# The inverse of a chunked scan by head groups, with its first products on four 64x64 tiles

## The reference

```
def step(S, inp):
    r_t, w_t, k_t, v_t, kk_t, b_t = inp
    sa = jnp.einsum('bhvk,bhk->bhv', S, -kk_t)
    S = (S * w_t[:, :, None, :] + sa[..., None] * b_t[:, :, None, :]
         + v_t[..., None] * k_t[:, :, None, :])
    y_t = jnp.einsum('bhvk,bhk->bhv', S, r_t)
    return S, y_t
```

## Time and profile before

| | |
|---|---|
| median of 3 runs | 1394.27 us (1393.8 to 1395.25) |
| profiled execution | 1393.7 us, its span 1391.9 us |
| busy, share of the span | PE 98%, weight loads 84%, DVE 68%, ACT 54%, POOL 5% |
| granted TensorE clock, mean | 0.999 of full speed |
| the scan's levels and joins | 101 to 135 us and 161 to 186 us |

### The profile page before, as it was taken

One profiled execution on the slowest core, in us unless ns is written; L12 is line 12 of the kernel. 1 busy time (PEld: TensorE's weight loads), 2 busy tenths in 40 slices (PEclk: granted clock), 3 DMA queues, 4 the chain that ended last, 5 costly groups with the idle time before them and its releaser, 6 DMA issues.

```text
span 1391.9 us, 23527 instructions
## 1 busy us (share of the span) xinstructions
PE 1363.1 (98%) x9838; PEld 1175.4 (84%) x9838; DVE 950.7 (68%) x1480; ACT 748.2 (54%) x1262; POOL 62.7 (5%) x63
## 2 busy tenths in 40 slices
PE   6999999999999999999999999999999999999998
PEld 6789888888889778888889877888888898788886
DVE  7896786766675776756667544577666697767665
ACT  6873434555456575545453446555555536555543
POOL 0003440000010000000000000000000100000000
PEclk9999999999999999999999999999999999999999
DMA  9421006555554415555565543545555653455551
GB/s 333 158 72 33 4 27 241 188 185 188 202 205 161 144 49 172 199 186 192 201 221 189 189 162 140 180 156 197 193 185 185 218 174 130 151 183 197 194 185 58
DMA packets 35291, 230.67 MB, mean 166 GB/s; under 512 B 4177, under 2 KB 5505, under 8 KB 8561
## 3 DMA queue, kind: packets, MB, share of 16 engines
q1 hardware_dynamic: 33376, 223.43, 46.6%
q0 software_dynamic: 1808, 5.74, 1.2%
HBM read 228.08 MB, written 1.05 MB: 165 GB/s over the span
## 4 chain that ended last, share of the span: by engine, by line
PE 92%; DVE 5%; ACT 2%; issue 0%; DMA 0%; SPq 0%; DVEq 0%; ACTq 0%
PE bank L1813 18%; PE bank L1814 17%; PE bank L1815 17%; PE bank L1938 17%; PE bank L1941 8%; PE bank L2205 3%; PE bank L1770 1%; PE bank L2011 1%; DVE wlo L999 1%; PE bank L2029 1%; PE bank L2045 1%; PE bank L2222 1%; DVE arena L1227 0%; PE bank L2383 0%; PE bank L2384 0%
## 5 line engine op out<-in xcount | busy, mean ns | idle before, releaser
L999 DVE TENSOR_TENSOR wlo<-raw,whi 128x1024 fp32r<-128x1024 f32 (+1 forms) x416 | 492.9, 1204 | 250.0 <-ACT whi L458 245.7
L458 ACT ACTIVATE whi<-raw 128x1024 fp32r<-128x1024 f32 (+1 forms) x416 | 425.5, 1041 | 329.3 <-PE bank L1815 231.7
L1813 PE MATMUL bank<-whi,XHL 128*128 128x512 f32 x872 | 342.3, 393 | 0.0
L1814 PE MATMUL bank<-wlo,XHL 128*128 128x512 f32 x872 | 339.6, 389 | 0.0
L1815 PE MATMUL bank<-whi,XHL 128*128 128x512 f32 x872 | 339.5, 389 | 0.0
L1938 PE MATMUL bank<-XHL,whi 128*128 128x512 f32 x1008 | 316.6, 395 | 0.2
L1941 PEld LDWEIGHTS bank<-XHL,wlo 128*128 128x128 f32 x1008 | 189.3, 188 | 44.5
L1941 PE MATMUL bank<-XHL,wlo 128*128 128x256 f32 x1008 | 198.1, 278 | 0.0
L1815 PEld LDWEIGHTS bank<-whi,XHL 128*128 128x128 f32 x872 | 163.7, 188 | 34.3
L1813 PEld LDWEIGHTS bank<-whi,XHL 128*128 128x128 f32 x872 | 163.7, 188 | 34.2 <-issue 1.7
L1814 PEld LDWEIGHTS bank<-wlo,XHL 128*128 128x128 f32 x872 | 163.8, 188 | 32.7 <-issue 0.5
(11 more groups left out here) (302 smaller groups left out, 1265.3 us busy)
## 6 DMA issues: line engine op xcount, KB each, us to landing
raw<-in_w_mlp SPq DMA_DIRECT2D x128, 1024.0 KB, 4.9
raw<-in_w_rv SPq DMA_DIRECT2D x8, 1024.0 KB, 4.9
raw<-in_w_rg SPq DMA_DIRECT2D x8, 1024.0 KB, 4.9
raw<-in_w_reo SPq DMA_DIRECT2D x8, 1024.0 KB, 5.0
raw<-in_w_k SPq DMA_DIRECT2D x4, 1024.0 KB, 9.6
raw<-in_w_v SPq DMA_DIRECT2D x4, 1024.0 KB, 9.8
raw<-in_w_r SPq DMA_DIRECT2D x4, 1024.0 KB, 4.9
raw<-in_w_rwo SPq DMA_DIRECT2D x4, 1024.0 KB, 5.0
```

Source lines behind the costliest of these rows:

```text
L458: act.activation(high, full, ACT.Copy).then_inc(hi_done, 1)
L999: dve.tensor_tensor(low, full, high, ALU.subtract).then_inc(lo_done, 1)
L1813: pe.matmul(out_, xh[xs], wh[ws], start=start, stop=False)
L1814: pe.matmul(out_, xh[xs], wl[ws], start=False, stop=False)
```

## The change

The heads are taken in two groups of eight neighbours (`q` = 0 and 1), each with four even and four odd heads, instead of even and odd halves.

- First products (`halves`): even heads as before, odd heads across, rows 0 to 63 to output partitions 64 to 127 and the reverse. So four tiles of the array are used. ACT copies even heads in one piece and odd heads in two, which puts the halves back: three copies for each group and level instead of one for each parity.
- The second group's first products stand behind the filler, not ahead of it, and both groups' inverse products behind one another. In the first level each group waits for both parities' seeds.
- DVE subtracts for both groups and then transposes, as before by halves; in level 4 it now finishes a group (`TI_`, then `TT_`) before the other.
- BONUS: four of the eight steps move from behind level 4 to behind level 2.
- Joins: the corner is kept for even heads on partitions 0 to 63 and for odd heads on 64 to 127. The first join goes by group, on two tiles, the first group's ahead of the first pair products; the second join for all heads, on two tiles, behind the bonus products.
- L2334 takes 64 rows of `TT_` for the first 64 tokens, where it took 128 with a zeroed half. `zero_tail` goes.

```
-        MBM = [[at(23296, 2, KT, HD), at(0, 2, KT, HD)], [at(1024, 2, KT, HD), at(9264, 2, KT, HD)]]
...
+        MBM = [[at(23296, 2, 2, 4, HD), at(0, 2, 2, 4, HD)], [at(1024, 2, 2, 4, HD), at(9264, 2, 2, 4, HD)]]
+        HALF_BANK, INVERSE_BANK, STEP_BANK, JOIN_BANK = ((4, 5), (6, 7)), (0, 1), (4, 6), (5, 7)
+        TOP, LOW = slice(0, HD), slice(HD, P)
...
                 for i in range(5):
-                    for f in range(2):
-                        act.wait_ge(half_prod, 10 * c + 2 * i + f + 1)
-                        act.activation(PM[c][:, f], psum[4 + f][:, :].rearrange("p (h s) -> p h s", h=KT), ACT.Copy)\
-                            .then_inc(half_ready, 1)
+                    for q in range(2):
+                        even, odd = (psum[b][:, 0:T].rearrange("p (h s) -> p h s", h=4) for b in HALF_BANK[q])
+                        act.wait_ge(half_prod, 10 * c + 2 * i + q + 1)
+                        act.activation(PM[c][:, q, 0], even, ACT.Copy).then_inc(half_ready, 1)
+                        for to, source in ((TOP, LOW), (LOW, TOP)):
+                            act.activation(PM[c][to, q, 1], odd[source], ACT.Copy).then_inc(half_ready, 1)
...
+                if c == 0:
+                    act.wait_ge(bonus_sum, 1)
+                    act.activation(rn, psum[5][:, 0:T], ACT.Copy).then_inc(bonus_copied, 1)
...
             def level(c, i, work):
 
-                for f in range(2):
-                    n = 10 * c + 2 * i + f
-                    rows = slice(0, P if i < 4 else HD)
+                rows = slice(0, P if i < 4 else HD)
+                for q in range(2):
+                    n = 10 * c + 2 * i + q
                     dve.wait_ge(inv_prod, n + 1)
-                    dve.tensor_tensor(TI_[rows, f], TI_[rows, f], bank8(6 + f)[rows], ALU.subtract).then_inc(inv_doubled, 1)
-                for f in range(2):
-                    if i < 4:
-                        dve.wait_ge(inv_doubled, 10 * c + 2 * i + f + 1)
-                        dve.transpose(TT_[:, f], TI_[:, f]).then_inc(doubled, 1)
-                    else:
-                        dve.wait_ge(step_prod, 2 * c + f + 1)
-                        dve.tensor_tensor(TT_[:, f], TT_[:, f], bank8(f), ALU.subtract).then_inc(doubled, 1)
+                    ti = flat(TI_[rows, q])
+                    dve.tensor_tensor(ti, ti, psum[INVERSE_BANK[q]][rows, :], ALU.subtract).then_inc(inv_doubled, 1)
+                    if i == 4:
+                        dve.wait_ge(step_prod, 2 * c + q + 1)
+                        tt = flat(TT_[:, q])
+                        dve.tensor_tensor(tt, tt, psum[STEP_BANK[q]][:, :], ALU.subtract).then_inc(last_doubled, 1)
+                if i < 4:
+                    for q in range(2):
+                        dve.wait_ge(inv_doubled, 10 * c + 2 * i + q + 1)
+                        dve.transpose(flat(TT_[:, q]), flat(TI_[:, q])).then_inc(doubled, 1)
                 work(i)
...
-                if i == 4:
-                    dve.wait_ge(rho_ready, 2)
+                for q in {2: (0,), 4: (1,)}.get(i, ()):
+                    dve.wait_ge(rho_ready, q + 1)
                     dve.wait_ge(kappa_ready, 1)
                     dve.wait_ge(lo_done, 2 * (U0["rwo"]))
-                    for p in range(KT):
+                    for p in range(4 * q, 4 * q + 4):
...
-            def zero_tail(c):
-
-                pool.wait_ge(t12_prod, 2 * c + 2)
-                pool.wait_ge(t22_ready, 2 * c + 2)
-                pool.memset(TT_[HD:P].rearrange("p f h s -> p (f h s)"), 0.0).then_inc(tail_zeroed, 1)
...
-                        ins = pe.matmul(psum[4 * c + f][0:HD, p * HD:(p + 1) * HD], BE[rows, p, ts], AR[rows, 2 * p + c, 0, HD:P],
+                        be, kap = BE[rows, p, ts], AR[rows, 2 * p + c, 0, HD:P]
+                        ins = pe.matmul(psum[4 * c][rows, p * HD:(p + 1) * HD], kap if f else be, be if f else kap,
                                         start=(p == 0), stop=(p == KT - 1))
...
+            BLOCKS = (TOP, LOW)
+
+            def both(bank, w, x, q, f, blocks=2):
+
+                for h in range(4):
+                    for blk in range(blocks):
+                        rows = BLOCKS[blk]
+                        ins = pe.matmul(psum[bank][rows, f * T + h * HD:f * T + (h + 1) * HD], w[rows, q, f, h],
+                                        x[rows, q, f, h], start=(h == 0 and f == 0), stop=(h == 3 and f == 1))
+                return ins
+
+            def halves(c, i, q):
+
+                keys = MBM[c][i % 2] if i else FIRST_KEYS[c]
+                if i == 0:
+                    pe.wait_ge(ti_ready, 2 * c + 2)
+                    pe.wait_ge(first_masked, 2 * c + 2)
+                    pe.wait_ge(corner_ready, c + 1)
+                    pe.wait_ge(beta_ready, 2 * c + 2)
+                    if c and q:
+                        pe.wait_ge(keys_ready, 4)
+                        pe.wait_ge(state_ready, 8)
+                else:
+                    pe.wait_ge(inv_doubled, 10 * c + 2 * (i - 1) + q + 1)
+                    pe.wait_ge(level_masked, 8 * c + 2 * (i - 1) + q + 1)
+                for h in range(4):
+                    for f in range(2):
+                        for blk in range(2):
+                            rows, o = BLOCKS[blk], BLOCKS[blk ^ f]
+                            ins = pe.matmul(psum[HALF_BANK[q][f]][o, h * HD:(h + 1) * HD], keys[rows, q, f, h],
+                                            TI_[rows, q, f, h], start=(h == 0), stop=(h == 3))
+                ins.then_inc(half_prod, 1)
+
+            def inverse(c, i, q):
+
+                for f in range(2):
+                    pe.wait_ge(half_ready, 30 * c + 6 * i + 3 * q + 2 * f + 1)
+                    if f == 0:
+                        if i:
+                            pe.wait_ge(doubled, 8 * c + 2 * (i - 1) + q + 1)
+                        else:
+                            pe.wait_ge(tt_ready, 2 * c + q + 1)
+                    ins = both(INVERSE_BANK[q], TT_, PM[c], q, f, 2 if i < 4 else 1)
+                ins.then_inc(inv_prod, 1)
+                if i == 4:
+                    for f in range(2):
+                        ins = both(STEP_BANK[q], PM[c], TT_, q, f)
+                    ins.then_inc(step_prod, 1)
+
+            def first_join(c, q):
+
+                pe.wait_ge(inv_doubled, 10 * c + 8 + q + 1)
+                pe.wait_ge(last_doubled, 2 * c + q + 1)
+                for h in range(4):
+                    p, cols = 4 * q + h, slice(h * HD, (h + 1) * HD)
+                    pe.matmul(psum[JOIN_BANK[q]][LOW, cols], CORNER[TOP, p], TI_[TOP, q, 0, h], start=(h == 0), stop=(h == 3))
+                    ins = pe.matmul(psum[JOIN_BANK[q]][TOP, cols], CORNER[LOW, p], TT_[LOW, q, 1, h], start=(h == 0),
+                                    stop=(h == 3))
+                ins.then_inc(p1_prod, 1)
+
+            def second_join(c):
+
+                pe.wait_ge(p1_ready, 2 * c + 2)
...
+                    q, h, cols = p // 4, p % 4, slice(p * HD, (p + 1) * HD)
+                    for f, w, x in ((0, JOIN[LOW, p], TT_[LOW, q, 0, h]), (1, TI_[TOP, q, 1, h], JOIN[TOP, p])):
+                        ins = pe.matmul(psum[6 + f][TOP, cols], w, x, start=(p == 0), stop=(p == KT - 1))
+                        if p == KT - 1:
+                            ins.then_inc(t12_prod, 1)
...
                 for i in range(5):
...
-                        both(4 + f, MBM[c][i % 2] if i else FIRST_KEYS[c], TI_, f).then_inc(half_prod, 1)
+                    halves(c, i, 0)
                     if c == 0 and i < 4:
...
-                        both(6 + f, TT_, PM[c], f, 2 if i < 4 else 1).then_inc(inv_prod, 1)
-                        if i == 4:
-                            both(f, PM[c], TT_, f).then_inc(step_prod, 1)
+                    halves(c, i, 1)
                     if c == 0 and i == 0:
                         next(r_second)
...
+                    for q in range(2):
+                        inverse(c, i, q)
+                first_join(c, 0)
+                pe.wait_ge(inv_doubled, 10 * c + 10)
...
                 pair_products(c, 0)
...
+                first_join(c, 1)
                 if c == 0:
-                    pe.wait_ge(bonus_prod, 1)
+                    pe.wait_ge(bonus_prod, 2)
+                    pe.wait_ge(p1_ready, 1)
...
+                second_join(c)
                 for g in range(4):
...
-                        pe.wait_ge(tail_zeroed, c + 1)
+                        pe.wait_ge(t12_ready, 2 * c + 2)
+                        pe.wait_ge(t22_ready, 2 * c + 2)
                     for h in range(4):
                         p, f = 2 * g + h // 2, h % 2
-                        for t, w in zip(TOKEN_HALVES, (TT_, PM[c])):
-                            ins = pe.matmul(psum[4][t, 256 + h * HD:256 + (h + 1) * HD], w[:, f, p],
-                                            SR[g % 2][:, h * HD:(h + 1) * HD], start=(h == 0), stop=(h == 3))
```

(55 more changed lines are left out.)

86 lines of the change are left out of this document (30 added, 56 removed).

## The result

The changed kernel takes 1403.06 us (median of 6 runs, 1400.74 to 1404.82), the kernel before 1394.04 (6 runs, 1393.24 to 1395.25): a ratio of 1.006, interval 1.005 to 1.0071. It is slower, as forecast, but 4 us beyond the forecast and 1 us beyond the range of 1387 to 1402. The profiled execution took 1401.09 us with a span of 1399.3, so 7.4 more than the kernel before in its span; the medians are 9.0 apart.

A forecast was written before the change was run, and what follows sets the result against it. TensorE was taken to bound the kernel, with a latency chain in the second chunk's new inverse. Terms -6.7 + 11.5 = +4.8 us on 1393.7 gave 1398.5, plus 0.6 for the median: 1399.0; 8-in-10 range 1387 to 1402.

The forecast's parts named there:

- Mixed shapes, +11.5: Pair loop, L2334 (new L2373): alternating 64x64 and 128x64 products cost +1.44 us a step, +11.5 us in eight steps.
- The upper of the two bounds: Pair loop: each change of tile shape waits 0.15 us for the array, so a product takes 0.26 us.
- no wait: Rival, 17%: separate tiles don't wait, the pair loop's mixed step stays at 0.52 us; 1387.6 us, faster.
- part of it: Rival, 10%: a shorter wait in the mixed step, +0.7 us a step, +5.8 in all; 1393.4 us, no difference.
- First products at the four-tile rate: Inverse: 16 first products take 0.47 us on four tiles, against 0.94 on two and 1.87 on one.
- the third rival: Rival, 5%: the inverse's first products run at the two-tile rate with the mixed step dear; 1403.9 us.
- First chunk, -3.5: First chunk's inverse: level period falls from 5.57 to 4.63 us and half of BONUS moves into level 2; -3.5 us together.
- The place where ACT would be late: First chunk, level 4: ACT's queued L458 and L530 items delay its copies, so PE waits 1.4 us.
- Second chunk, -3.2: Second chunk's inverse: period falls from 3.81 to 3.47 us, later levels 3.6 and 3.9; masks end sooner, -3.2 us.
- The median, +0.6 over the profiled execution: Whole kernel: the median of runs stands 0.6 us above the profiled execution, taking 1398.5 to 1399.0 us.
- -6.7: Inverse in both chunks: total gain forecast at 6.7 us, with a range of 5 to 9.

The follow-up runs named there:

- The version with 128 rows: The changed kernel with the sa step's first-64-token products over all 128 rows again and POOL zeroing the lower half: 1392.66 us, ratio 0.9979 to the kernel before.

## Why the prediction was right in direction and short in size

By the starts in the two profiles, the first `sa` step of the first chunk comes 3.0 us earlier, its pair loop is 5.6 longer, from its end to the second chunk's first products is 0.1 longer, from there to that chunk's first `sa` step 1.2 shorter, and its pair loop 5.7 longer: +7.2 us, which is the 7.25 by which all that follows is late. Of the 4 us between forecast and median, 2.0 are the second chunk's, 1.4 the median's, and 0.5 the first chunk's; the rest is rounding and small terms.

- **Mixed shapes, +11.5: measured +11.3.** The upper of the two bounds, from a change of shape between tiles that don't overlap, was the right one, and with it the sign. The three runs on it leave no room for the first two rivals (no wait, part of it).
- **First products at the four-tile rate: right**, which ends the third rival. The rule of the Trainium skill that would have halved the rate ("TensorEngine Tiling (Array Packing)", Gotcha 1) doesn't show here: each of L2234's banks is written from both row tiles, and 16 products last 0.69 us.
- **First chunk, -3.5: measured -3.0.** Level period 4.71 for 4.63. The masks end 3.3 us earlier (135.28 against 138.60); 0.3 goes because all 16 passes of the right-hand side now stand behind the second join and start at 135.31, where four were left behind the masks. The place where ACT would be late was named and is there, 1.1 us on PE for the 1.4 forecast. The forecast's own terms add up to 1.9 at PE's end (2.8 + 0.94 - 0.45 - 1.4), not 1.75, which changes little. What was not seen is that PE's gap has a price of its own, below.
- **Second chunk, -3.2: measured -1.2. This is the step that failed.** The levels were put at 3.47, 3.47, 3.6 and 3.9 us, 14.4 in all; they took 16.2. The text named VectorE's group-norm steps but let them cost the later levels 0.1 and 0.4, and left the centring step its 1.2 us. In the kernel before they took 0.91, 1.34, 1.47 and 1.21 us, each what POOL's instruction had left and 0.55 us more. The change moved the levels, so the steps met POOL's instructions with 1.0 to 1.2 us of them left instead of 0.4 to 0.9, took 1.57 to 1.79 us, and the subtractions and masks stood behind them. Two runs show it: without POOL beside it the step takes 0.65 us and its level 3.62, and with seven of eight heads left out the first `sa` step comes 27.45 us after the first products instead of 28.72, 1.3 of the 2.0 us. The forecast makes it 29.9 - 3.2 = 26.7. What is left lies in the levels: 0.6 in the third, where the cut step still waits for POOL, and 0.4 in the first two, ahead of any long step. There the trace of the changed kernel has ScalarE in the chain: three copies take 1.21 us a group for the 1.0 of the forecast (168.11 to 169.32), and the second group's last inverse products start at 170.57, right behind the last copy's end at 170.52. No run tests that part.
- **The median, +0.6 over the profiled execution: 2.0 measured** (1403.06 against 1401.09). The forecast took the distance from the kernel before. Closing the gap in level 4 took 0.0024 off the ratio, 3.3 us, of which the profiles of the two show 1.4 in the scan. That the rest is a stretch at 1.2 GHz behind this gap, in part of the executions, is inferred from the clocks of the executions and from that run: the changed kernel's one profile shows none. The version with 128 rows, with the same levels, shows it directly, but its clock falls near 920 us too, so a stretch at another place of the changed kernel is not ruled out.

The sum in place of -6.7 + 11.5 = 4.8 is -3.0 + 0.1 - 1.2 + 11.3 = 7.2 us.

## What to carry to other kernels

A matmul cut to the rows that it needs is not cheaper if its neighbours keep another shape: count the changes of shape in the order of issue, and either pay for zeroed rows or put equal shapes together. When a change shortens a chain of latencies, look again at each instruction that stands in another engine's queue between two links: its duration in the old trace holds only for what ran beside it there. Here it could be read off that trace: what GpSimd's instruction under way had left, and 0.55 us. A short gap on TensorE can cost more than its length, so closing it may be worth more than the profile's wait says.

## What the runs showed of the hardware that was not expected

- In the version with 128 rows, behind a stretch with PE busy 0.81 of 2.00 us, the granted clock stood at 0.62 and 0.53 in the next two windows of 2 us, and at 1.00 in the one behind. Not each execution has it: at the same place the changed kernel's profile has 0.87 of 2.00 and then 1.00.
- Group-norm steps of 128x512 on VectorE, both operands in SBUF, ended 0.55 us behind the end of the POOL instruction that was under way at their start, in the profiles of before and after and of the runs above, wherever they met one. Alone they took 0.65 to 0.69.
- VectorE's product of 64 elements a partition, both operands in SBUF, took up to 1.11 us beside POOL. The subtractions, with one operand in PSUM, took 0.67 to 0.69 whether POOL worked or not.
